# Convolution taps split at token 369, and a projection woven into a scan, in a two-layer token mixer with gathered experts

## The reference

```python
def conformer_conv(u):
    a, g = jnp.split(u, 2, axis=-1)
    y = depthwise_conv(a * jax.nn.sigmoid(g), conv_w, conv_b)      # CONV_K = 31 taps over the tokens
    return jax.nn.silu(layernorm(y, conv_ln_g, conv_ln_b))

def mlstm_inputs(u):
    qk, v, o, gates = split_cols(u, (2 * BR_W, BR_W, BR_W, MLSTM_GATES))
    qk = jax.nn.silu(depthwise_conv(qk, mlstm_conv_w, mlstm_conv_b))   # 3 taps
    ...
# mlstm_scan, one chunk of 128 tokens (4 heads of 128, forwards and backwards)
    s = jnp.einsum('bhid,bhjd->bhij', qc, kc) * jnp.exp(logw - m_t[..., None])
    num = jnp.einsum('bhij,bhjd->bhid', s, vc) + w_prev[..., None] * jnp.einsum('bhid,bhde->bhie', qc, cmat)
    ...
    cmat = decay[..., None, None] * cmat + jnp.einsum('bhjd,bhje->bhde', kw, vc)

def block(xb):                                  # PEER experts: 128 tokens at a time
    ...                                         # 8 heads x 16 chosen experts = 128 per token
    u_sel = jnp.take(u, expert, axis=0)
    v_sel = jnp.take(v, expert, axis=0)
    act = jax.nn.gelu(jnp.einsum('nd,nhkd->nhk', xb, u_sel).astype(jnp.float32), approximate=False)
    return jnp.einsum('nhk,nhkd->nd', (gate * act).astype(dt), v_sel)
```

## Time and profile before

| what | us |
|---|---|
| median of 3 runs | 5880.32 (5867.57 to 5884.21) |
| the profiled execution | 5877.57, span 5875.8 |
| TensorE busy | 4020.7 (68%), mean granted clock 0.776 |
| VectorE busy | 3199.4 (54%) |
| GpSimd busy | 2779.7 (47%) |
| ScalarE busy | 700.2 (12%) |

### The profile page before, as it was taken

The page is one execution under the profiler, slowest core; times in us unless marked ns, Lnnn a source line. Parts: engine busy times, 40 slices in busy tenths (PEclk is TensorE's granted clock), DMA queues, the critical chain, the costliest instruction groups (busy, mean ns, idle before and its releaser), DMA issues.

```text
span 5875.8 us, 64032 instructions
## 1 busy us (share of the span) xinstructions
PE 4020.7 (68%) x23448; PEld 2399.3 (41%) x23448; DVE 3199.4 (54%) x7529; ACT 700.2 (12%) x1475; POOL 2779.7 (47%) x2602
## 2 busy tenths in 40 slices
PE   7889776777998964554456677888897544334446
PEld 5677543335565842221124434456685400000001
DVE  5421688567624885756644404645378775664430
ACT  2310122114000001000000001233200100000000
POOL 0000143566432445777776761000024677777775
PEclk9999888879999986665567888899999755555556
DMA  7545575899987989999999994121469999999999
GB/s 274 199 169 164 180 247 182 284 326 324 318 289 264 357 325 340 385 372 397 362 405 406 405 400 167 39 56 49 136 231 368 339 390 392 403 363 402 409 405 374
DMA packets 628584, 1747.51 MB, mean 297 GB/s; under 512 B 84344, under 2 KB 182520, under 8 KB 626608
## 3 DMA queue, kind: packets, MB, share of 16 engines
q0 software_dynamic: 379904, 1384.47, 62.0%
q1 hardware_dynamic: 216880, 302.74, 15.5%
q10 hardware_dynamic: 31488, 56.23, 2.7%
HBM read 1711.16 MB, written 32.07 MB: 297 GB/s over the span
## 4 chain that ended last, share of the span: by engine, by line
DMA 17%; PE 13%; issue 12%; POOL 9%; DVE 8%; ACT 1%; POOLq 0%; ACTq 0%; DVEq 0%
DMA arena<-in_peer_v,arena 11%; POOL arena L3367 9%; DMA arena<-in_peer_u,arena 5%; PE bank L850 3%; PE bank L1381 2%; DVE arena L2438 2%; PE bank L1424 2%; PE bank L1303 1%; PE bank L861 1%; PE bank L1325 1%; DVE arena L1725 1%; PE bank L1353 1%; PE bank L1255 1%; PE bank L946 1%; DVE arena L2302 0%
## 5 line engine op out<-in xcount | busy, mean ns | idle before, releaser
L3367 POOL DMA_INDIRECT arena<-in_peer_u,arena x1280 | 1431.0, 1118 | 1981.8 <-DVE arena L2328 843.6
L2438 DVE CUSTOM_DVE_ANT_0 arena<-arena 128x1024 f32<-128x1024 f32 x1280 | 1541.1, 1222 | 990.6 <-DMA arena<-in_peer_u,arena 974.6
L1424 PE MATMUL bank<-arena 128*32 128x256 f32 x10240 | 1113.0, 532 | 1234.9 <-DMA arena<-in_peer_v,arena 1229.5
L3367 POOL DMA_INDIRECT arena<-in_peer_v,arena x1280 | 1324.2, 1035 | 702.0 <-PE bank L1424 340.3
L1424 PEld LDWEIGHTS bank<-arena 128*32 128x32 f32 x10240 | 252.1, 127 | 2042.2 <-DMA arena<-in_peer_v,arena 1900.4
L850 PE MATMUL bank<-arena 128*128 128x512 f32 (+1 forms) x1600 | 637.4, 551 | 38.0 <-DVE arena L1949 10.4
L1303 PE MATMUL bank<-arena 128*128 128x256 f32 x2560 | 624.9, 405 | 21.3 <-DVE arena L2277 12.3
L1303 PEld LDWEIGHTS bank<-arena 128*128 128x128 f32 x2560 | 513.9, 204 | 134.5 <-issue 49.9
L850 PEld LDWEIGHTS bank<-arena 128*128 128x128 f32 x1600 | 317.4, 205 | 305.8 <-issue 287.7
L1381 PE MATMUL bank<-arena 128*128 128x256 f32 x1280 | 295.9, 393 | 33.4 <-DVE arena L2199 21.2
L1325 PE MATMUL bank<-arena 128*128 128x256 f32 x1280 | 289.3, 383 | 11.3 <-ACT arena L3078 4.5
(11 more groups left out here) (278 smaller groups left out, 3772.1 us busy)
## 6 DMA issues: line engine op xcount, KB each, us to landing
arena<-in_w_in SPq DMA_DIRECT2D x152, 1024.0 KB, 9.5
arena<-in_mod_w POOLq DMA_DIRECT2D x20, 2048.0 KB, 12.0
arena<-in_peer_wq SPq DMA_DIRECT2D x40, 1024.0 KB, 6.4
arena<-in_w_branch SPq DMA_DIRECT2D x30, 1024.0 KB, 5.4
arena<-in_w_out SPq DMA_DIRECT2D x20, 1024.0 KB, 7.1
arena<-in_peer_u,arena POOLq DMA_INDIRECT x1280
arena<-in_peer_v,arena POOLq DMA_INDIRECT x1280
arena<-in_w_branch SPq DMA_DIRECT2D x20, 512.0 KB, 8.0
```

What stands on the lines that cost most here:

```text
L1424: i = mm(banks[6 + g // 2][32 * j:32 * j + 32, (g % 2) * W:(g % 2 + 1) * W], G["ws"][:, g, 32 * m:32 * m + 32], G["row"][ROW_BUFFER["v", i ...
L2438: v.tensor_tensor_reduce(u, u, G["h2"][it % 2], 1.0, 0.0, ALU.mult, ALU.add, G["dots"][:, n:n + 1]).then_inc(*pr.step("dot", it, n))
L3367: fl.done(eng.indirect_dma_start(G["row"][x], None, table, bass.IndirectOffsetOnAxis(ids[:, n:n + 1], 0)), f"row_landed{x}", (kind + "_lan ...
```

## The change

For layer 1, the taps of tokens 0 to 368 (all whose 31 neighbours lie in tokens 0 to 383) are computed in `opening`, on VectorE: those of the first half of the channels between the two halves' projections, those of the second half at the end. The taps of tokens 369 to 511 stay where all taps were. `opening`'s share goes from 1.0 to 1.6. Since the early taps write to where the incoming rows of layer 1 lay, token block 3 comes into another buffer.

For layer 0's latents, `mls(p, 1)` is woven into `mls_scan(p, 0)`, and the stage `mls1` is gone. The second half's keys, values and padded input get places of their own: the buffers of the expert's residual rows (`XS`) and scores (`SCO`), and the place of the convolution's output. So VectorE waits until the second block's experts are chosen, and the first block's residual rows are loaded at slot 104 instead of 24, after `mlss1` has ended.

```diff
 def pass_stages(p):
-    s += ["rows", "mlss0", "mls1", "mlss1", "attn"] + ["conv"] * late(p)
+    s += ["rows", "mlss0"] + ["mls1"] * (not late(p)) + ["mlss1", "attn"] + ["conv"] * late(p)
...
+def taps_ready(p):
+
+    return token_parts(p)[0][1] - TAPS // 2 if p is L1 else 0
...
         def norm_rows(p, x):
 
+            if p is L1 and x == p.n // P - 1:
+                return norm_work()[1][:, 0, :]
             return norm_work()[0][:, x % 2, :]
...
         def mls_work(p, h=0):
+            if late(p) and h:
+                k, v_, pad = XS[:, 0:2 * p.n], SCO[:, 0:nb * 2 * E1], MA[:, 0:2 * (p.n + 2)]
...
             # normed(), on each of tensor, vector and scalar
-                yield from mls_scan(p, 0)
-                yield from mls(p, 1)
+                if late(p):
+                    yield from weave(mls_scan(p, 0), mls(p, 1), units(p)["mls"] / units(p)["scan"])
+                else:
+                    yield from mls_scan(p, 0)
+                    yield from mls(p, 1)
...
             # on each of tensor, vector and scalar
-            side_by_side("o1", opening(L1), side, SLOTS - LEAD, 1.0)
+            side_by_side("o1", opening(L1), side, SLOTS - LEAD, 1.6)
...
             def opening(p):                                   # vector
                 yield from conv_part(p, 0)
+                conv_taps(p, 1, 0, TAPS, early=True)
+                yield 0
...
             def conv_part(p, part):                           # vector
                 for h in range(2):
+                    if h and hi < p.n:
+                        conv_taps(p, 0, 0, TAPS, early=True)
...
-            def conv_taps(p, h, part, size=8):
+            def conv_taps(p, h, part, size=8, early=False):
-                eng.wait_ge(*at("conv_glu", p.name, h, len(token_parts(p)) - 1))
+                lo, hi = (0, taps_ready(p)) if early else (taps_ready(p), p.n)
+                eng.wait_ge(*at("conv_glu", p.name, h, 0 if early else len(token_parts(p)) - 1))
...
-                            v.scalar_tensor_tensor(y[:, m, :], cp[:, m, j:j + p.n], tap, y[:, m, :], ALU.mult, ALU.add)\
+                            v.scalar_tensor_tensor(y[:, m, lo:hi], cp[:, m, j + lo:j + hi], tap, y[:, m, lo:hi], ALU.mult, ALU.add)\
...
             def mls(p, h):                                    # tensor, vector, scalar
-                if h and not woven(p):
+                if h and not (woven(p) or late(p)):
                     mn.stage((f"mls{h}", p.name))
...
             def mls(p, h):                                    # vector
-                if h == 0 or woven(p):
+                if h == 0 or woven(p) or late(p):
+                    if late(p) and h:
+                        eng.wait_ge(*at("experts", PC0.first + 1))
                     v.memset(M["pad"], 0.0).then_inc(*mn.step("mpad0", pn, h))
...
                 def x_in(it):                                 # scalar
                     if it > 0:
                         eng.wait_ge(*at("x_stored", it - 1))
+                    else:
+                        for e in ENG:
+                            eng.wait_ge(*at("end", e, ("mlss1", "l0")))
...
-                            if n == 24:
+                            if n == (104 if it == 1 else 24):
                                 x_in(it - 1)
...
             def x_rows_in(p, xs):                             # sync
-                    if x >= 2:
+                    if p is L1 and x == p.n // P - 1:
+                        eng.wait_ge(*at("full", ("xT", p.name, t - 1, 1)))
+                    elif x >= 2:
                         eng.wait_ge(*at("xn", p.name, t - 2))
```

More of the change, by code:

```diff
@@ L964, in opening @@
                 yield from conv_part(p, 0)
+                yield 0.1
             def rest(p):
@@ L1516, in _ @@
             costs = []
-            side_by_side("o1", opening(L1), side, SLOTS - LEAD, 1.0, costs)
+            side_by_side("o1", opening(L1), side, SLOTS - LEAD, 1.6, costs)
             fl.marks[("cost", "o1")] = costs
@@ L1720, in conv_taps @@
                         if j == 0:
-                            v.tensor_scalar(y[:, m, :], cp[:, m, j:j + p.n], tap, cb[:, m:m + 1], ALU.mult, ALU.add)\
+                            v.tensor_scalar(y[:, m, lo:hi], cp[:, m, j + lo:j + hi], tap, cb[:, m:m + 1], ALU.mult, ALU.add)\
                                 .then_inc(*mn.step())
@@ L1724, in conv_taps @@
                             eng.wait_ge(*mn.latest(1 if j % size else 0))
-                            v.scalar_tensor_tensor(y[:, m, :], cp[:, m, j:j + p.n], tap, y[:, m, :], ALU.mult, ALU.add)\
+                            v.scalar_tensor_tensor(y[:, m, lo:hi], cp[:, m, j + lo:j + hi], tap, y[:, m, lo:hi], ALU.mult, ALU.add)\
                                 .then_inc(*mn.step())
                 eng.wait_ge(*mn.latest())
-                fl.mark(("conv_mean", p.name), mn.sem)
+                if not early:
+                    fl.mark(("conv_mean", p.name), mn.sem)
             def conv_tail(p):
```

## The result

The change is slower: 5899.35 us median of 20 runs against 5879.44 us of 20 runs of before, ratio 1.0032, 95% interval 1.0023 to 1.0042. I had forecast 5861 us, in a range of 5838 to 5890. The profiled execution has a span of 5901.8 us, 26.0 more than before.

The account below looks back on a forecast made before the run. No engine bounds throughout; each stretch was priced by its own limit (DVE, PE or POOL's gathers). Left-over taps -16, gathers +9 and weave -10 sum to -17 us from 5877.6 us: 5861 us, range 5838 to 5890.

Parts of the forecast that it names:

- the cost of the early taps on the gathers: Last v rows of layer 0: 0.23 us more per gather over some 45 rows, 9 us lost, bounds 0 and 30.
- the signs of being wrong: Last v rows growing by over 20 us, or the woven stretch taking 165 us again or under 135.
- That the taps fit on DVE: Beside layer 0's last v rows: 124 early taps, 67 us, fit in nearly empty DVE and cost its own time nothing.
- The weave: Layer 0's second projections woven into the first mLSTM scan: 10 us won, bounds 7 lost and 36 won.
- the 8 and 2 of the sum: Weave gains: 8 us up to the first v row, where DVE limits; 2 us after it, where gathers limit.
- that sign: PE busy above 85% in the first woven stretch, where it was 54 of 70 us.
- Rivals 2, 3 and 4: Woven stretch not gather-held: 5845 us, 0.11; weave hidden by waits: 5871 us, 0.20; five PSUM banks delay v rows: 5890 us, 0.15.
- The left-over taps: Layer 1's mixer: taps over 143 tokens in place of 512, 16 us won, bounds 2.4 and 21 + 2.4.
- The barrier: At 3598.38 us PE waits 5.37 us for DVE's first eight taps; these shrink to 2.6, 2.4 us won.
- the mixer behind it: Layer 1, 3665 to 3735 us: DVE gives up 21 us of taps; 13.6 of PE's 16.1 us waits won.
- The small pieces at nothing: Row block 3 of layer 1 landing in another buffer, with the next weights queued behind its load: 0.
- Rival 1: Gathers beside layer 0's last v rows are not slowed by the early taps: -26, 5852 us, chance 0.14.

Follow-up runs that it names:

- runs_of_8: The change, with every fourth tap pair of the early taps waiting for the tap before it, giving runs of 8 taps; 5849.73 us, ratio 0.9953.
- weave_only: The change without the early taps and with the share at 1.0; the weave and the moved load stay; 5868.64 us, ratio 0.9982.
- runs_of_2: As runs_of_8, but every early tap pair waits for the tap before it, a break behind each tap; 5846.60 us, ratio 0.9940.
- reduce_run: The change with 120 early taps made one-input maximum reductions in unbroken runs of 62, early sums left out; 5848.15 us, ratio 0.9941.

## Why the prediction was wrong

**The step that failed** is the cost of the early taps on the gathers: 9 us taken, bounds 0 and 30, about 52 measured. It is also the first of the signs of being wrong that I had named: last v rows longer by over 20 us. The rate came from 38 gathers beside layer 0's taps. Those taps wait for their predecessor at every fourth pair (the calls there pass a size of 4), so they run in eights, and their gathers take at most 1.49 us. The change calls with all 31 pairs, in which no tap waits for the one just before it. I multiplied a rate per gather and never asked what breaks the taps up, though both calls stand in the code. The upper bound failed too: the gathers beside dots also get breaks, for around that row DVE idles 1.3 to 2.8 us between two dots. With runs as long as those of the row, in runs_of_8, the gathers take 12.1 us more than in before, and the table's last v gather of layer 0 loses 5.4 us against the 26th of its block; the 9 lie between. That the taps fit on DVE was right: they took 63 us, 67 forecast. The trace of before could not show a hold; the difference in length between the two runs could be read, and should have widened the range to a run's whole length: two runs of 32 us.

**The weave** was right in size, in part by luck: -10.0 us in weave_only, 10 forecast, but from other pieces than the 8 and 2 of the sum. The rows that answer to the earlier trace rows, shifted by the 2.6 us that this execution is late (busy us by engine as above, clock, DMA share, GB/s):

```profile
1005.60:1067.00 61.40, 43.26 (x183) 30.23 (x185) 51.21 (x123) 14.36 (x32) 27.09 (x23) 0.83 0.68 223
1067.00:1166.00 99.00, 73.22 (x378) 34.72 (x378) 53.31 (x130) 22.38 (x41) 61.37 (x61) 0.83 0.97 340
1166.00:1260.00 94.00, 58.77 (x389) 35.39 (x390) 64.90 (x179) 23.46 (x52) 55.53 (x52) 0.69 0.85 300
```

The first v sum comes after 61.4 us (62 forecast, 71.7 before): 10.3 won. From there to the second scan's first matmul it took 99.9 us, 96.4 before: 3.5 lost, where I had 2 won. PE is busy 73 us there in place of 81, so taking PE work out gave nothing; that the gathers hold the stretch fits this, at a DMA share of 0.97 as before. The second scan, in 67.8 us in place of 70.2, gave 2.4 that I had at nothing, and ends 6.6 us earlier than before. PE is busy 70% in the first stretch, not above 85%: that sign was wrong, since only 43 of the 57 us of PE work that I counted moved there. Rivals 2, 3 and 4 did not happen.

**The left-over taps** returned more than the 16 us taken. The barrier gave 2.7 us (2.4 forecast). With PE's matmuls paired in order, the mixer behind it gave 18.8 (13.6 taken, 21 the bound): 18.2 up to the 3735.3 us of before, 0.6 just behind. The taps over 143 tokens, DVE's group from 3705 to 3800 us, answering to the earlier trace rows:

```profile
L1743 DVE SCALAR_TENSOR_TENSOR arena<-arena 128x143 f32<-128x143 f32 x60 | 18.0, 363 | 1.0
```

60 fill 18.0 us, 0.30 each; I had 0.33. Where the 18.2 us come from is seen on PE, over the same 209 matmuls in before and in the change (the stretch's row as above, then the 128x512 matmuls and the waits that are left):

```profile
3664.00:3735.30 71.30, 54.34 (x209) 36.05 (x209) 63.95 (x134) 13.71 (x32) 0.00 (x0) 0.89 0.12 34
L850 PE MATMUL bank<-arena 128*128 128x512 f32 x53 | 26.8, 651 | 0.0
```

```profile
3702.60:3755.70 53.10, 48.36 (x209) 32.52 (x209) 39.80 (x129) 13.13 (x30) 0.00 (x0) 1.00 0.15 47
L859 PE MATMUL bank<-arena 128*128 128x512 f32 x53 | 23.9, 593 | 0.0
L1044 PE MATMUL bank<-arena 128*128 128x128 f32 x24 | 3.4, 278 | 2.3 <-DVE arena L1830 2.3
L1063 PE MATMUL bank<-arena 128*128 128x128 f32 x12 | 1.9, 281 | 1.5 <-DVE arena L1861 1.5
```

PE's waits for DVE fell from the 16.1 us of the earlier trace rows to 3.8, by 12.3, a little under the 13.6 taken. The other 6 us are matmuls that got faster: the granted clock was 0.89 in before, partly at 1.2 GHz in a stretch in which PE waited up to 8 us at a time, and 1.00 in the change, where its longest wait is 2.3 us. The sum had nothing for the clock. The 25 us in the table hold 3.3 more: from the last gather's start to PE's last sum of v rows it is 10.1 us in place of 13.4.

**Sum of the terms as measured:** 10 won, 52 lost, 25 returned, in the profiled execution; with 2.5 us of late start and the 6.7 us of drift that is +26. The small pieces at nothing were not tried alone; weave_only has the moved load and the other buffer in it. Rival 1, gathers not slowed, is what reduce_run (without the early sums) and nearly runs_of_2 show: 5848 and 5847 us, near its 5852. The change loses to before only by its unbroken runs; with a break at least every eight taps it beats before by 0.5 to 0.6%.

## What to carry to other kernels

Before long DVE work is laid beside transfers that POOL issues, count how many instructions follow each other without a wait between them, those with two SBUF inputs above all: a mean per gather, taken where DVE's work is broken up, says nothing of an unbroken run. A wait of an instruction for the one just before it costs DVE 0.13 us here; two such waits in every eight taps gave back nearly all of the 52 us. And look at the longest instruction of a group, not at its mean alone.

## What the runs showed of the hardware

A gather beside 60 DVE instructions with two SBUF inputs was held to their end (26.9 and 28.95 us), beside one-input ones at 0.38 us each too (20.7 us), beside reductions of the same 369 values, 0.45 us each, not at all (0.94 us). After a break two gathers of 1.2 us pass before the next is held; why these two still pass the runs don't show.
